# Down projections of a two-block network: the two products with the upper weights done as one pass of 512 elements

## What the kernel computes

```python
FFN_HIDDEN = ((-(-8 * D_MODEL // 3)) + 255) // 256 * 256     # 2816
D_FF = 4 * D_MODEL                                           # 4096

def swiglu(h, w1, w3, w2):
    return (jax.nn.silu(h @ w1) * (h @ w3)) @ w2
...
    h = h + g2 * swiglu(hn, ffn_w1[layer], ffn_w3[layer], ffn_w2[layer])     # layers 0 and 1
...
    x = x + jnp.square(jax.nn.relu(h2 @ w_up[l])) @ w_down[l]               # second block
```

## Time and profile before

| what | value |
|---|---|
| median of 3 runs | 1251.72 us (1245.33, 1251.72, 1254.25) |
| profiled execution, its own time | 1253.79 us |
| its span, first to last instruction | 1252.0 us |
| mean granted TensorE clock | 0.964 of full speed |
| PE busy | 1175.9 us (94%) |
| DVE busy | 815.5 us (65%) |
| ACT busy | 590.6 us (47%) |
| chain that ended last, PE's share | 82% |

### The profile page before, as it was taken

The page is one execution under the profiler, slowest core; times in us unless marked ns, Lnnn a source line. Parts: engine busy times, 40 slices in busy tenths (PEclk is TensorE's granted clock), DMA queues, the critical chain, the costliest instruction groups (busy, mean ns, idle before and its releaser), DMA issues.

```text
span 1252.0 us, 24371 instructions
## 1 busy us (share of the span) xinstructions
PE 1175.9 (94%) x10460; PEld 1119.1 (89%) x10460; DVE 815.5 (65%) x1487; ACT 590.6 (47%) x1085; POOL 77.7 (6%) x94
## 2 busy tenths in 40 slices
PE   5888799999996999999997999998999999999999
PEld 2687689999995999999997888887998999899999
DVE  3874759988885566554454578887764575777543
ACT  2434546445445444444444466763333355556442
POOL 0000010000011000000100001111520001000000
PEclk9889999999998999999698899998999999999999
DMA  9660638898891647642244242221212555755520
GB/s 389 266 256 2 258 146 346 342 357 319 333 349 43 232 170 274 202 172 69 72 182 171 75 142 70 102 102 68 70 37 85 185 183 188 272 199 202 185 107 13
DMA packets 32363, 226.41 MB, mean 181 GB/s; under 512 B 3584, under 2 KB 4736, under 8 KB 5120
## 3 DMA queue, kind: packets, MB, share of 16 engines
q1 hardware_dynamic: 30528, 221.20, 47.6%
q10 hardware_dynamic: 1728, 3.67, 0.8%
HBM read 223.80 MB, written 1.05 MB: 180 GB/s over the span
## 4 chain that ended last, share of the span: by engine, by line
PE 82%; DVE 9%; ACT 5%; DMA 2%; issue 1%; POOL 0%; SPq 0%; DVEq 0%; ACTq 0%; POOLq 0%
PE bank L546 21%; PE bank L548 20%; PE bank L547 20%; DVE sb_wlo L1772 3%; ACT sb_whi L1302 2%; PE bank L989 2%; PE bank L651 1%; PE bank L584 1%; DVE sb_ring L1806 1%; DMA sb_ring<-in_f 1%; PE bank L574 1%; DMA sb_ring<-in_ada 1%; PE bank L564 1%; PE bank L1011 1%; PE bank L980 1%
## 5 line engine op out<-in xcount | busy, mean ns | idle before, releaser
L546 PE MATMUL bank<-sb_xh,sb_whi 128*128 128x256 f32 x1496 | 427.7, 286 | 8.1 <-DVE sb_wlo L1772 5.6
L547 PE MATMUL bank<-sb_xl,sb_whi 128*128 128x256 f32 x1496 | 420.8, 281 | 0.0
L548 PE MATMUL bank<-sb_xh,sb_wlo 128*128 128x256 f32 x1496 | 420.6, 281 | 0.0
L1772 DVE TENSOR_TENSOR sb_wlo<-sb_ring,sb_whi 128x1024 fp32r<-128x1024 f32 (+1 forms) x201 | 244.2, 1221 | 140.5 <-ACT sb_whi L1302 139.8
L546 PEld LDWEIGHTS bank<-sb_xh,sb_whi 128*128 128x128 f32 x1496 | 286.3, 191 | 16.7 <-issue 12.6
L547 PEld LDWEIGHTS bank<-sb_xl,sb_whi 128*128 128x128 f32 x1496 | 288.0, 192 | 0.1
L548 PEld LDWEIGHTS bank<-sb_xh,sb_wlo 128*128 128x128 f32 x1496 | 286.1, 191 | 0.0
L1302 ACT ACTIVATE sb_whi<-sb_ring 128x1024 fp32r<-128x1024 f32 (+1 forms) x201 | 210.7, 1052 | 95.0 <-PE bank L548 84.1
L1772 DVE TENSOR_TENSOR sb_wlo<-sb_more,sb_whi 128x1024 fp32r<-128x1024 f32 x108 | 131.0, 1223 | 72.9 <-ACT sb_whi L1302 72.9
L548 PE MATMUL bank<-sb_hh,sb_wlo 128*128 128x256 f32 x608 | 168.7, 277 | 0.0
L546 PE MATMUL bank<-sb_hh,sb_whi 128*128 128x256 f32 x608 | 168.7, 277 | 0.0
(11 more groups left out here) (349 smaller groups left out, 1863.8 us busy)
## 6 DMA issues: line engine op xcount, KB each, us to landing
sb_more<-in_w SPq DMA_DIRECT2D x34, 1024.0 KB, 6.8
sb_ring<-in_w SPq DMA_DIRECT2D x32, 1024.0 KB, 5.9
sb_ring<-in_adaT SPq DMA_DIRECT2D x26, 1024.0 KB, 7.7
sb_ring<-in_f SPq DMA_DIRECT2D x24, 1024.0 KB, 4.9
sb_more<-in_adaT SPq DMA_DIRECT2D x18, 1024.0 KB, 9.1
sb_ring<-in_gn SPq DMA_DIRECT2D x8, 1024.0 KB, 4.9
sb_ring<-in_gd SPq DMA_DIRECT2D x8, 1024.0 KB, 4.9
sb_ring<-in_up SPq DMA_DIRECT2D x8, 1024.0 KB, 5.8
```

The source lines that it names most:

```text
L546: te.matmul(out, wh, rh, start=start, stop=False, skip_group_check=skip)
L547: te.matmul(out, wh, rl, start=False, stop=False, skip_group_check=skip)
L548: return te.matmul(out, wl, rh, start=False, stop=stop, skip_group_check=skip)
L1772: ve.tensor_tensor(lo, x, hi.bitcast(F32), ALU.subtract).then_inc(*lo_dve.up(n))
```

## The change

The hidden data of the upper and the lower part become one buffer `hs` (`hs2`), `[128, 2, NH, T]`, of which `hh` and `hl` are the halves. For feature tiles 0 to 6 of each down projection the first two passes of a set become one: the weights-upper block is loaded once and 512 elements are moved, 256 of the upper and 256 of the lower part, which lie 22 KB apart (32 KB in the second block). The result fills the whole PSUM bank: columns 0 to 255 hold the product with the upper part, 256 to 511 that with the lower part. The third pass, weights-lower by data-upper, adds to columns 0 to 255 as before. VectorE then adds both halves of the bank to `h`, in two instructions, of which the second waits for the first. Tile 7 keeps the three passes and the single add. The buffers keep their size and their start; `gap` is unchanged.

```diff
-        hh = sb("hh", [128, NH0, T], F32R)
-        hl = sb("hl", [128, NH0, T], F32R)
+        hs = sb("hs", [128, 2, NH0, T], F32R)
+        hh, hl = hs[:, 0, :, :], hs[:, 1, :, :]
...
+            def mm2(out, wh, wl, r, start, stop):
+                te.matmul(out, wh, r, start=start, stop=False)
+                return te.matmul(out[:, 0:T], wl, r[:, 0, :], start=False, stop=stop)
+
+            def mm1(out, wh, wl, r, start, stop):
+                return mm3(out[:, 0:T], wh, wl, r[:, 0, :], r[:, 1, :], start, stop)
...
-                        end = mm3(ps[:, 0:T], hi[:, c], lo[:, c], hh[:, k, :], hl[:, k, :], k == 0, k == NH0 - 1)
+                        end = (mm2 if j < 7 else mm1)(ps[:, :], hi[:, c], lo[:, c], hs[:, :, k, :], k == 0, k == NH0 - 1)
...
-                    end = mm3(ps[:, 0:T], hi[:, c], lo[:, c], hh2[:, k, :], hl2[:, k, :], k == 0, k == NH2 - 1)
+                    end = (mm2 if j < 7 else mm1)(ps[:, :], hi[:, c], lo[:, c], hs2[:, :, k, :], k == 0, k == NH2 - 1)
...
+            def residual2(norm, j, step, gate):
+                if j == 7:
+                    residual(norm, j, step, gate)
+                    return
+                V.wait_ge(*pe.at(*step, j))
+                ps = ps_of((*step, j))
+                ve.scalar_tensor_tensor(h[:, j, :], ps[:, T:2 * T], gate, h[:, j, :], ALU.mult, ALU.add).then_inc(*dve.up())
+                V.wait_ge(*dve.now())
+                ve.scalar_tensor_tensor(h[:, j, :], ps[:, 0:T], gate, h[:, j, :], ALU.mult, ALU.add).then_inc(*dve.up(("h", norm, j)))
...
-                    residual(after, j, ("down", layer), mods[:, layer, 40 + j:41 + j])
+                    residual2(after, j, ("down", layer), mods[:, layer, 40 + j:41 + j])
...
-                ve.tensor_tensor(h[:, j, :], h[:, j, :], ps_of(("mdown", j))[:, 0:T], ALU.add).then_inc(*dve.up(("out", j)))
+                ps = ps_of(("mdown", j))
+                if j < 7:
+                    ve.tensor_tensor(h[:, j, :], h[:, j, :], ps[:, T:2 * T], ALU.add).then_inc(*dve.up())
+                    V.wait_ge(*dve.now())
+                ve.tensor_tensor(h[:, j, :], h[:, j, :], ps[:, 0:T], ALU.add).then_inc(*dve.up(("out", j)))
```

More of the change, by code:

```diff
@@ L458, in program @@
         gap(1, 128)
-        hh2 = sb("hh2", [128, NH2, T], F32R)
-        hl2 = sb("hl2", [128, NH2, T], F32R)
+        hs2 = sb("hs2", [128, 2, NH2, T], F32R)
+        hh2, hl2 = hs2[:, 0, :, :], hs2[:, 1, :, :]
         close()
```

## The result

The changed kernel takes 1255.3 us in the median of 20 runs (1251.63 to 1260.64), the kernel before 1250.2 us in 20 runs (1239.94 to 1255.71). The ratio is 1.0052, with a 95% interval of 1.0033 to 1.0070 (the two medians alone would give 1.0041): slower by half a per cent, where 0.56% faster was forecast. The profiled execution took 1260.25 us, its span is 1258.4 us and its mean clock 0.961 of full speed.

A forecast was written before the change was run, and what follows sets the result against it. The prediction took TensorE's stream (PE) to bound the changed stretches. Shorter sets save 4.0 us in layer 0 and second block plus 3.0 in layer 1, 7.0 together, other terms 0: 1244.7 us, range 1238 to 1254.

The forecast's parts named there:

- The passes: Down projections: a 512 pass takes 216 ns, the 256 pass stays at 113.3 (layer 1 117.7); 7.0 us less together.
- The upper bound of the prediction: Down projections: a pass of 512 takes at most 226.7 ns, 235.4 in layer 1.
- the excess goes with the elements: Rival, down projections: time above one element per cycle doubles with the longer pass; 0 to 1.3 us saved; chance 0.12.
- The spacing is drawn anew: Rival: changed rhythm hands the next stage, an up projection, another steady spacing; 2.9 us lost or 4.2 gained; chance 0.08.
- The jump: Rival, 512 pass: reading restarts between its two data runs, up to 87 ns each; 1290.4 us at 86 ns; chance 0.06.
- VectorE late: Rival, layer 0 down projection: VectorE makes lower weights too late; 3.9 us lost of 7.0, 1248.6 us; chance 0.04.
- more than the sum: Rival, down projections: excess hangs on crowding loads, the 256 pass falls to 106.7 ns; 12.7 us saved, 1239.0; chance 0.12.
- the second add: Down projections, VectorE: 21 extra adds, 0.48 to 0.56 us each, hidden by cover; cost 0.
- the weights' DMA, the bank and the tail: Down projections: layer 0's weight transfer, the PSUM bank held 0.5 us longer and the stage ends; cost 0.

The follow-up runs named there:

- the first ten kernels: The kernel before, the changed kernel and the first eight follow-up kernels, each traced once; no single time for the group.

## Why the prediction was wrong

**The failed step is "The passes".** It took 216 ns for a pass of 512, from L858, and left the pass of 256 at 113.3 (117.7 in layer 1), on the ground that the load beside it can't begin sooner. Measured are 235 and 118, in all three stages: a set of 353 ns where 329.3 and 333.7 were forecast. No run shows that the load sets the length of the short pass. In layer 0's trace of before a load's record, 188 ns long, even ends 78 ns behind the start of the pass that uses it. The upper bound of the prediction, that the excess goes with the elements, is what holds with the data at 64: the first long pass of a stage takes 0.22 us, twice 113, and all later ones twice 117.7. The Trainium skill's rule that the prediction weighed ("TensorE: Matmul & The Clock Gate", section "Back-to-back issue gap"), which the page gives for the isolated gap of two warm matmuls, makes 512 / 2.4 + 2.5 = 215.8 ns, and the trace disagrees with it here as it did for 256. L858 was the wrong neighbour. It is a plain float32 product, whose record of 256 elements takes 215.8 ns where a float32r pass of 256 takes 113.3; that its 2.5 ns above 213.3 carry over to a float32r pass of 512 was an assumption, and the half clock of the earlier trace rows could not support it, since there is no excess at all to be divided. So the forecast of 7.0 us fell to nothing.

**Below nothing it went by a rival whose place was wrong.** "The spacing is drawn anew" was priced for stages that the change doesn't touch, with a chance of 0.08, and never for the changed stages themselves. There it costs 176 x 13 ns in layer 0 and 256 x 13 ns in the second block, 2.3 + 3.3 = 5.6 us, and nothing in layer 1, which had the longer spacing already in the trace of before (in executions in which it had not, 2.3 us more). The range ended at 1254 because each rival was priced alone; two came together, the excess that goes with the elements (0.12, and no saving by itself) and the longer spacing. No chance stood for the two at once.

**The jump** was the one rival on the slower side; adjacent runs are as slow (352.9 ns), so its mechanism is refuted, although its sign came true. **VectorE late** and **more than the sum** are refuted by a PE without idle time and by sets of 353.

**Right** were: TensorE's stream sets the length of all three stretches; the second add is hidden; the weights' DMA, the bank and the tail cost nothing; there are two steady spacings at one clock and one code.

**The load as the partner of the excess** is made likely, not shown. The excess depends on the distance of data and weights modulo 256 bytes, and it fell when loads and outputs were halved together. The Trainium skill, in "TensorE: Matmul & The Clock Gate", section "LDWEIGHTS (loading the stationary operand)", has a load take time by its columns, not by its rows: 64 columns less would be 53 ns, an estimate from its figure, and the two rows differ by 188 - 134 = 54. Were the load all, though, a long pass with one load beside its 512 elements would carry no more than a short one. It carries twice as much. What else reads or waits beside the pass is open.

**Open** is also what picks the spacing behind a break. At the four breaks of L1245 the spacing changed over every time, 60 times in 60, but that is one kind of break. In single traces transposes led from the shorter to the longer (three stages), from the longer to the shorter (two kernels), or left the longer in place (three tiles), and a stream of long passes was followed by the shorter one. Only the entry by a long pass among short ones gave the longer one in every trace that had its data at 64 modulo 256, whichever spacing it came from.

## What to carry to other kernels

Read what a matmul pass costs from the distance between starts, and take the price of a longer one only from a row of the same type: here, with the data where they were, two passes in one moved the same elements in no less time. An unexplained excess over the elements is a reason to try the start of the data against the weights first, since that decided whether the merging paid at all. When a stream runs in the better of two steady spacings, an odd instruction in its midst is a risk to the whole stage behind it, and is to be priced in the stage that is changed. Compare spacings over several executions, and where the longer one is common try a cheap disturbance: two transposes gave 0.3 to 0.4% here, for a reason that isn't fully known.

## What the runs showed of the hardware

- float32r passes at the full granted clock of 1.00 (2.4 GHz) have two steady spacings with one code and one set of addresses: 113.3 and 117.7 ns for 256 elements. Layer 1's up projection, which none of the first ten kernels changes, ran in the longer one in five of their traces and in the shorter in five. Each kernel left one trace, so that one kernel changes from run to run is likely but not shown; if it does, it is 4.2 + 2.3 = 6.5 of the 15.8 us between the fastest and the slowest run of the kernel before.
- The spacing changes over at each of the four breaks of L1245, from either side, 60 times in 60 in the fifteen traces with both kinds of weights at 128 modulo 256 bytes; with both at 192 it is 118.7 ns on both sides.
- With the data at 64 and the weights at 128 a pass of 512 takes 226 ns behind passes of the shorter spacing and 235 in the stream, no less per element than the short ones around it. With the data at 0 or 128 it takes 230, where two short ones take 240.
- The distance of data and weights modulo 256 bytes changes the time of a set at the same clock and count: with three passes 340 or 353 ns at one distance and some 360 at another, with a long pass 346 to 353. Nothing waits in the profile while this happens; PE reads as fully busy.
